# First layer's scan: the output gate of groups 1 to 7 computed as a chain of seven quarter products instead of two full ones

## The reference

```
for l in range(2):                       # 1024 features, 256 + 256 tokens in layer 0
    q, k, v, z, xBC, dt, ga, gs = split(h @ w_in[l])
    x, B, C = silu(dwconv(xBC, conv_w) + conv_b)
    y = ssd_forward(x, dt_f, B, C) + ssd_backward(x, dt_b, B, C) + D * x
    ssd = rmsnorm(y * silu(z), g) @ w_ssd_o        # z: the output gate
```

## Time and profile before

| | |
|---|---|
| median of 3 runs | 2643.51 us (2640.7 to 2645.01) |
| the profiled execution | 2640.4 us, its span 2638.6 us |
| TensorE busy | 98% of the span |
| the first layer's scan | about 446 to 860 us |
| one group of it, where steady | 51.35 us |

### The profile page before, as it was taken

The page is one execution under the profiler, slowest core; times in us unless marked ns, Lnnn a source line. Parts: engine busy times, 40 slices in busy tenths (PEclk is TensorE's granted clock), DMA queues, the critical chain, the costliest instruction groups (busy, mean ns, idle before and its releaser), DMA issues.

```text
span 2638.6 us, 40130 instructions
## 1 busy us (share of the span) xinstructions
PE 2594.3 (98%) x15290; PEld 2042.5 (77%) x15290; DVE 1602.3 (61%) x2659; ACT 788.6 (30%) x1824; POOL 1187.0 (45%) x942
## 2 busy tenths in 40 slices
PE   8999999999999999999999999999999999999998
PEld 7779994555555777888778888876666688899998
DVE  1547835777778577887669660226766744666253
ACT  2430113665656333200021210014555422201210
POOL 4018970333323545457414554401221254586885
PEclk9999999999999999999999999999999999999999
DMA  9347666434341223343455533264443222387654
GB/s 286 97 118 207 183 200 171 112 89 112 105 111 41 57 77 84 95 116 96 110 167 171 157 88 88 88 180 122 108 111 102 65 80 72 88 222 218 169 169 120
DMA packets 519311, 333.12 MB, mean 126 GB/s; under 512 B 15328, under 2 KB 485712, under 8 KB 518864
## 3 DMA queue, kind: packets, MB, share of 16 engines
q1 hardware_dynamic: 507888, 298.19, 40.3%
q0 software_dynamic: 10784, 31.46, 4.8%
q10 hardware_dynamic: 448, 0.89, 0.1%
HBM read 328.11 MB, written 2.38 MB: 125 GB/s over the span
## 4 chain that ended last, share of the span: by engine, by line
PE 92%; DVE 3%; issue 1%; ACT 1%; PEld 1%; DVEq 1%; POOL 0%; PEldq 0%; DMA 0%; ACTq 0%
PE ps L1890 44%; PE ps L1526 24%; PE ps L2263 4%; PE ps L2260 2%; PE ps L2044 2%; PE ps L2021 2%; PE ps L2187 1%; PE ps L2213 1%; PE ps L2081 1%; PE ps L2246 1%; PE ps L2060 1%; PE ps L2069 1%; PE ps L2358 1%; PE ps L1846 1%; PE ps L1552 1%
## 5 line engine op out<-in xcount | busy, mean ns | idle before, releaser
L1526 PE MATMUL ps<-xnT,W 128*128 128x512 f32 (+1 forms) x1760 | 650.6, 525 | 1.8 <-DVE xnT L2516 0.8
L1526 PEld LDWEIGHTS ps<-xnT,W 128*128 128x128 f32 x1760 | 330.0, 190 | 291.1 <-issue 263.7
L929 POOL TENSOR_TENSOR W<-W 128x512 f32<-128x512 f32 x154 | 214.0, 1390 | 612.1 <-DMA W<-in_w_mlp 243.9
L1890 PE MATMUL ps<-TMP,W 128*128 128x128 f32 (+1 forms) x2848 | 482.2, 319 | 1.3 <-DVE TMP L2751 1.2
L1890 PEld LDWEIGHTS ps<-TMP,W 128*128 128x128 f32 x2848 | 422.9, 191 | 32.9 <-DVE TMP L2751 1.3
L1890 PE MATMUL ps<-BIG,W 128*128 128x128 f32 (+1 forms) x2736 | 437.2, 314 | 0.0
L1890 PEld LDWEIGHTS ps<-BIG,W 128*128 128x128 f32 x2736 | 391.4, 191 | 26.7 <-issue 0.7
L1890 PE MATMUL ps<-xnT,W 128*128 128x128 f32 (+1 forms) x2032 | 324.2, 311 | 0.0
L1890 PEld LDWEIGHTS ps<-xnT,W 128*128 128x128 f32 x2032 | 288.7, 191 | 18.9 <-issue 0.8
L1038 ACT ACTIVATE TMP<-ps 128x512 f32<-128x512 f32 (+3 forms) x205 | 91.0, 449 | 569.2 <-PE ps L1890 392.4
L931 POOL TENSOR_TENSOR W<-W 128x512 f32<-128x512 f32 x154 | 219.9, 1428 | 27.4 <-issue 6.0
(11 more groups left out here) (397 smaller groups left out, 3374.5 us busy)
## 6 DMA issues: line engine op xcount, KB each, us to landing
W<-in_w_in SPq DMA_DIRECT2D x188, 512.0 KB, 4.4
W<-in_w_mlp SPq DMA_DIRECT2D x128, 512.0 KB, 4.1
W<-in_ada_w SPq DMA_DIRECT2D x96, 512.0 KB, 4.1
BIG<-cs_rows POOLq DMA_DIRECT2D x96, 256.0 KB, 4.8
W<-in_w_ssd_o SPq DMA_DIRECT2D x32, 512.0 KB, 5.2
W<-in_w_gate SPq DMA_DIRECT2D x22, 512.0 KB, 6.3
W<-in_w_up SPq DMA_DIRECT2D x22, 512.0 KB, 4.5
W<-in_w_down SPq DMA_DIRECT2D x16, 512.0 KB, 3.8
```

Source lines behind the costliest of these rows:

```text
L929: nc.gpsimd.tensor_tensor(w1[:, 0:K, :], wb[:, 0:K, :], wb[:, K:2 * K, :], ALU.add)
L1526: last = mm(dst, w[:, c, 0:m], rhs(k), start=k == 0, stop=k == total - 1)
L1890: done = mm(PS[bank][:, third + half * H:third + half * H + H], w[:, at + c, :], x[:, c, :], start=first and opens and c == 0, stop=last a ...
```

## The change

For layer 0 and groups 1 to 7 the two full products z0 and z1 become seven products of four matmuls each, on token halves and feature halves, 256 columns wide. TensorE runs steps 1 and 2 behind `states(g, 2)`, steps 6, 5 and 7 behind C, and steps 4 and 3 behind `outputs(g, 3)`. B goes where z0 was, and waits for the same convolution. The products use PSUM banks 4 and 5, so the x transposes of the next `turned` wait until these are read. ScalarE copies bank 4 out four times (`gate_copied`) and then takes the silu of both halves in place (`gate_closed`), before `finish(g)`. VectorE adds bank 5 three times (`gate_added`), the last time ahead of the gating of group g's output. GpSimd makes the four weight sums of the next group behind its second DMA of each group (7 times), and once, ahead of the first of them, four sums of token quarters (`gate_tokens`), which are kept where `hT` stands. So the whole of `hT` is written out to DRAM, early in the scan, and its first half is read back too. Each of the seven groups takes two more slots of the ring.

```diff
 def front_order(l, g):
-    return (0, 1, 4, 2, 3, 5) if early_z(l, g) else range(6)
+    return (0, 1, 2, 4, 5, 3) if chained_z(l, g) else range(6)
...
+def gate_keys(g):
+
+    return [("ssd", 0, g, "z0"), ("ssd", 0, g, "z1"), ("zsums", g, 0), ("zsums", g, 1)]
...
-                if key == ("att", 0, 0, "q"):
+                if key == ("ssd", 0, 1, "C"):
                     sp.wait_ge(n_x, scaled_until("down1", KC - 1, 1))
-                    sp.dma_start(h_dram[:, :, :], hT[:, 4:8, :]).then_inc(h_out, 16)
+                    sp.dma_start(h_dram[:, :, :], hT[:, :, :]).then_inc(h_out, 16)
+                if key == quick_keys(MERGE[0] + 6)[0]:
+                    sp.wait_ge(z_ad, gate_adds(NG - 1, 3))
+                    sp.dma_start(hT[:, 0:4, :], h_dram[:, 0:4, :]).then_inc(h_in, 16)
...
+                def gate_tokens():
+
+                    b11, b12, b21, b22 = (xnT[:, 4 * f:4 * f + 4, S * m:S * m + S] for f in range(2) for m in range(2))
+                    t1, t2, t4, t3 = t_gate
+                    pool.wait_ge(n_sh, 8 * NORMS["down1"])
+                    pool.wait_ge(h_out, 16)
+                    nc.gpsimd.tensor_tensor(t1, b12, b11, ALU.subtract).then_inc(z_t, 1)
+                    pool.drain()
+                    nc.gpsimd.tensor_tensor(t2, b22, t1, ALU.subtract).then_inc(z_t, 1)
+                    pool.drain()
+                    nc.gpsimd.tensor_tensor(t4, b21, t2, ALU.subtract).then_inc(z_t, 1)
+                    nc.gpsimd.tensor_tensor(t3, b22, b12, ALU.subtract).then_inc(z_t, 1)
...
+                        if i == 1 and chained_z(l, g + 1) and g < NG - 1:
+                            if g == 0:
+                                gate_tokens()
+                            pool.drain()
+                            sums_of_weights(gate_keys(g + 1), 4, z_ws)
+                            pool.drain()
...
+                def gate_copied(g, step):
+                    gate_done(act, g, step)
+                    if g >= 2 and step == 1:
+                        R("y1", 2 * (g - 2) + 2)
+                    i, m = {1: (0, 0), 6: (0, 1), 7: (1, 1), 4: (1, 0)}[step]
+                    copy(gate_out(g, i, m), PS[4][:, 0:S]).then_inc(z_cp, 1)
+
+                def gate_closed(g):
+                    act.wait_ge(z_cp, gate_copies(g, 4))
+                    act.wait_ge(z_ad, gate_adds(g, 3))
+                    for t in range(2):
+                        z_of = zs[:, g % 2, t, :]
+                        A(z_of, z_of, ACT.Silu).then_inc(ssd["gated"], 1)
...
@@ -1361,28 +1424,39 @@
                     if more:
                         center(g + 1, 0)
                         center(g + 1, 1)
-                        if l == 0:
-                            gated(g + 1, 0)
-                            activated(g + 1, 0)
                     else:
                         R("skip", 2 * NG)
                         keep(0, "q")
                     if l == 0:
                         decays(g, 2)
+                        if more:
+                            center(g + 1, 2)
+                            gate_copied(g + 1, 1)
                         decays(g, 3)
                     if not more:
                         keep(0, "k")
                         keep(0, "v")
-                    if more:
+                    if more and l == 0:
+                        center(g + 1, 3)
+                        gate_copied(g + 1, 6)
+                        activated(g + 1, 0)
+                        activated(g + 1, 1)
+                        gate_copied(g + 1, 7)
+                        activated(g + 1, 2)
+                        gate_copied(g + 1, 4)
+                        activated(g + 1, 3)
+                        if g == NG - 2:
+                            below(NG - 1, 0)
+                        gate_closed(g + 1)
+                    elif more:
                         center(g + 1, 2)
...
+                        for t in range(2):
                             gated(g + 1, t)
...
@@ -1974,19 +2048,54 @@
...
                 def front(g, t, ready=None):
-                    b = 0 if early_z(l, g) and t == 5 else t % 2
-                    if early_z(l, g) and t == 4:
-                        R("conv", 4 * g + 1)
-                    elif early_z(l, g) and t == 5:
-                        R("conv", 4 * g + 3)
-                    elif early_z(l, g) and t == 2:
-                        R("gated", 2 * g + 1)
-                    elif t >= 2:
+                    if t >= 2:
                         R("conv", 4 * g + t - 1)
+                    elif g and chained_z(l, g - 1):
+                        R("conv", 4 * (g - 1) + t + 3)
                     elif g:
-                        R("gated", 2 * (g - 1) + (2 if early_z(l, g - 1) else t + 1))
+                        R("gated", 2 * (g - 1) + t + 1)
                     n = T if t < 3 else nt
-                    product([("ssd", l, g, FRONT[t])], PS[b][:, 0:n], lambda k: xnT[:, k, 0:n], ready=ready)
...
+                    if step == 1:
+                        R("xcd", 3 * g)
+                        R("xc", g)
+                        tile(ka)
+                        times(X, wa[:, 0:4, :], b11, opens=True).then_inc(z_pe, 1)
+                    elif step == 2:
+                        times(Y, wa[:, 4:8, :], b21, opens=True).then_inc(z_pe, 1)
+                    elif step == 6:
+                        pe.wait_ge(z_ws, g)
+                        pe.wait_ge(z_t, 2)
+                        pe.wait_ge(z_cp, gate_copies(g, 1))
+                        give(times(X, w1[:, 4:8, :], t2), ka)
+                    elif step == 5:
+                        pe.wait_ge(z_ad, gate_adds(g, 2))
+                        give(times(Y, w1[:, 0:4, :], t1, opens=True), k1)
+                    elif step == 7:
+                        pe.wait_ge(z_t, 4)
+                        pe.wait_ge(z_cp, gate_copies(g, 6))
+                        times(X, wb[:, 0:4, :], t3).then_inc(z_pe, 1)
+                    elif step == 4:
+                        pe.wait_ge(z_cp, gate_copies(g, 7))
+                        give(times(X, wb[:, 4:8, :], t4), kb)
+                    else:
+                        pe.wait_ge(z_ad, gate_adds(g, 7))
+                        give(times(Y, w2[:, 0:4, :], b22), k2)
...
                 def turned(g):
...
+                    if chained_z(l, g):
+                        pe.wait_ge(z_cp, gate_copies(g, 4))
+                        pe.wait_ge(z_ad, gate_adds(g, 3))
...
@@ -2136,7 +2248,7 @@
                     if more:
                         front(g + 1, 1)
                         if l == 0:
-                            front(g + 1, 4)
+                            front(g + 1, 2)
...
-                    if more:
+                    if more and l == 0:
+                        gate(g + 1, 1)
+                        gate(g + 1, 2)
+                        front(g + 1, 3)
+                        gate(g + 1, 6)
+                        gate(g + 1, 5)
+                        gate(g + 1, 7)
...
                     outputs(g, 1 if l else 3)
-                    if more:
-                        if l:
-                            front(g + 1, 4)
+                    if more and l == 0:
+                        gate(g + 1, 4)
+                        gate(g + 1, 3)
...
+                def gate_added(g, step):
+                    gate_done(dve, g, step)
+                    dve.wait_ge(z_cp, gate_copies(g, {2: 1, 7: 7, 3: 6}[step]))
+                    i, m = {2: (0, 0), 7: (1, 1), 3: (0, 1)}[step]
+                    whole = gate_out(g, i, m)
+                    V.tensor_tensor(whole, PS[5][:, 0:S], whole, ALU.add).then_inc(z_ad, 1)
...
                     if l == 0:
                         masked(g, 2)
+                        if more:
+                            gate_added(g + 1, 2)
                         masked(g, 3)
                     elif not more:
...
                     if more:
                         conv(g + 1, 2)
+                        if l == 0:
+                            gate_added(g + 1, 7)
                         conv(g + 1, 3)
...
                         R("ychunk", n_ch * (g + 1))
                         y = yz[:, 2 * g + t, 0:nt]
                         V.tensor_tensor(y, y, PS[2 + t][:, 0:nt], ALU.add)
+                    if more and l == 0:
+                        gate_added(g + 1, 3)
                     dve.drain()
                     for t in range(2):
                         y = yz[:, 2 * g + t, 0:nt]
```

More of the change, by code:

```diff
@@ L246, with chained_z, gate_copies, gate_adds @@
 FRONT = ("x0", "x1", "B", "C", "z0", "z1")
-def early_z(l, g):
+def chained_z(l, g):
     return l == 0 and g > 0
 def front_order(l, g):
-    return (0, 1, 4, 2, 3, 5) if early_z(l, g) else range(6)
+    return (0, 1, 2, 4, 5, 3) if chained_z(l, g) else range(6)
+def gate_keys(g):
+    return [("ssd", 0, g, "z0"), ("ssd", 0, g, "z1"), ("zsums", g, 0), ("zsums", g, 1)]
+def gate_copies(g, step):
```

(56 more changed lines are left out.)

7 lines of the change are left out of this document (3 added, 4 removed).

## The result

The changed kernel took 2646.07 us (median of 22 runs, 2642.32 to 2648.38) beside 2642.90 us for the kernel before on the same chips: a ratio of 1.0013, interval 1.0007 to 1.0019. So it is slower by 3.2 us, clear of the noise of these runs but less than the 0.2% set above, and 0.8 us above the forecast of 2645.3. The sum came out well; several of its terms did not, and in both directions.

The account below looks back on a forecast made before the run. TensorE, busy throughout a steady group, was taken as the bound, with an equally long chain from the gate's end. Group 0 +4.05, steady groups -3.9, last group +1.6: +1.8 on 2643.5 gives 2645.3 us; 8-in-10 range 2636 to 2652.

Parts of the forecast that it names:

- TensorE's work: Gate product in each of 7 groups: seven narrower products take 12.09 us instead of 13.74, a gain of 1.65 us.
- rival D: Each step of the gate product's chain restarts TensorE, 0.3 us each, seven a group: 14 us more, 2659; chance 0.10.
- The chain at the gate's end: Groups 1 to 6, after the gate's last product: finish and B's wait come 1.0 us later (0.5 to 1.6).
- The weight sums, cover 1.3 us, cost nothing: GpSimd's four sums, groups 1 to 6: mask ready near 634.6, wanted by outputs(g, 1) at 635.9, so no cost.
- rival C: Weight sums hold VectorE in every group, outputs(g, 1) waits 1.8 us six times: in all +12.6 us, 2656; chance 0.12.
- The token sums, +5.7 us in group 0: GpSimd's token and weight sums delay VectorE's masks once, so outputs(0, 1) stalls 5.7 us (0 to 8).
- rival A: GpSimd's sums in group 0 hold VectorE less long, the 5.7 us stall falls away: 2639.6 us; chance 0.15.
- The last group, +1.6 us: Group 7: finish 2.1 us later behind below and two silus, 0.5 us slack, tail 1.6 us later (0.7 to 2.1).

Follow-up runs that it names:

- the spill alone: The kernel before, with only the residual written whole to DRAM and its first half read back six jobs into the merge: 2644.09 us, ratio 0.9999.

## Why the prediction held, and where its terms did not

**TensorE's work** was right. It forecast 1.65 us less in each group; the group without waits lasts 49.46 us, against 51.35 less z0's wait of 0.26 in the kernel before, which is 1.63. No step of the chain restarted TensorE for long (rival D): in the steady groups no wait stands at a line of the gate.

**The chain at the gate's end** was right in size and incomplete in mechanism. I took 1.0 us. B comes 1.25 us late by the trace, where 0.26 + 1.0 was forecast, and its weight load's wait grew by 1.08. By the experiments a group gets 0.33 + 1.00 = 1.33 us back with the whole chain gone, of which 0.26 were there before: 1.07. But I had written that the addition ahead of the multiplications costs nothing more. That holds only while the Silus stand beside it. Alone they were worth 0.33 us, and the addition's place the other 1.00.

**The weight sums, cover 1.3 us, cost nothing** was the step that failed in the steady groups. It rested on sums that begin behind the DMA, 16.6 us into the group (625.8 - 609.25), with 2.3 us of them on VectorE's two-operand operations. The drain kept them until 20.8 us into it (627.79 - 607.02), all four met the masks or the operation behind them and cost 4.0 us, and the cover was overrun: 0.58 us a group, by taking the drain away and by leaving the sums out alike. Over six groups this is 3.5 us that the sum lacked, and why the steady groups gained nothing instead of 3.9 us. The prediction had named a wait at `outputs(g, 1)` as a sign that it is wrong, and that sign came. It is the mechanism of rival C at a third of its size; its length of a sum (2.2 us) was wrong, 1.3 to 1.4 here, and what pushed it over the edge was their place.

**The token sums, +5.7 us in group 0**, failed the other way: no stall, rival A's outcome. But A's reason (VectorE gets several operations in at each drain) held in full at the first drain only. Beside sums with nothing between them VectorE got one operation in for each sum, and mostly two where 0.14 us or more lay between them. Filling that one gap brought a stall of 4.9 us and the group up by 7.2. So the pattern was read nearly rightly and the gap of 2.71 us overlooked, which is as long as ten mask operations. How narrow it was: in the kernel without the second drain the gap was 2.29 us, and a wait of 1.5 came back (group 0 at 51.17). Why the gap differs between kernels (2.26 to 2.71 us) is not shown.

**The last group, +1.6 us**: measured 1.76, made of 0.62 us at the q product, 1.01 and 0.19 at masks, less small change. The forecast had the q product's wait only as its lower bound (0.7) and took 1.6 at the copy that sets the tail; what came on top fell on waits for masks. Its `finish` is 2.6 us behind, as forecast.

**The sum.** Forecast for the scan +1.8 us; measured -1.3 in group 0, nothing in the steady groups, +1.8 in the last: +0.5. Of the two missed terms (5.4 us too dear in group 0, 3.9 too cheap in six groups) most cancels. The kernels' difference is 3.2 us where +1.8 was forecast, and 2.7 of it lie where the forecast had nothing. So the forecast of 2645.3 was near in good part by luck.

**Behind the scan** the forecast had nothing. The second step of attention takes 0.95 us longer in both traces. VectorE there, in the changed kernel:

```profile
854.21 2.16 DVE L3139 TENSOR_TENSOR BIG<-xnT 128x1024 f32<-128x1024 f32 x1
```

GpSimd there, in the changed kernel and then in the kernel before, where the same operation of VectorE started at 854.41 and took 1.22 us:

```profile
852.12 1.75 POOL L960 TENSOR_TENSOR W<-W 128x512 f32<-128x512 f32 x1 [1.00 <-issue]
854.01 1.27 POOL L962 TENSOR_TENSOR W<-W 128x512 f32<-128x512 f32 x1
```

```profile
853.13 1.38 POOL L929 TENSOR_TENSOR W<-W 128x512 f32<-128x512 f32 x1 [1.37 <-issue]
854.65 2.10 POOL L931 TENSOR_TENSOR W<-W 128x512 f32<-128x512 f32 x1
```

GpSimd's next weight sums begin 2.1 us ahead of it now and 1.3 us ahead before, so that VectorE comes second where it came first. Without the drain in the scan the operation takes 1.63 us and the step 8.3 with the same spill, and with the spill alone 1.22 and 7.90, so it is the phase of the two engines and not the traffic. That leaves 3.2 - 0.5 - 0.95 = some 1.7 us of the median's difference, which itself is known to 1.6 us either way. Medians less scan and second step spread over 2.2 us among all kernels here without order. The stretch at half clock in attention could carry it: the two steps that hold it are together 1.9 and 2.0 us longer in the traces of the changed kernel than in the kernel before. But they are 1.6 us longer with the spill alone too, whose median did not move. So this is not shown and stays open.

## What to carry to other kernels

Before a wait is called covered, follow where in time each operation of the other engine will really stand, drains included: a cover of 1.3 us was lost to a start four us later than assumed. When work is taken off a chain, look for the second way of nearly the same length beside it: the close of the gate was worth 0.33 us alone and 1.33 with the addition's place. Here three small edits in three queues (two of them moves, one a drain left out), with the same arithmetic, turned a change that lost 3 us into one that gains 0.33% (2634.55 us beside 2644.01, five runs, ratio 0.9954 to 0.9979).

## What the runs showed of the hardware

A GpSimd drain behind the issue of its own DMA took 4.11 us here (3.01 when one sum of 1.28 us had been put between), though the profile shows no other GpSimd operation in it; without such a DMA ahead it took 0.16 to 0.31. VectorE operations with two SBUF operands beside back-to-back GpSimd operations of 1.3 us lose one us to each of these, and beside five GpSimd operations, two of 2.4 us and three of 1.3, the eight masks took 9.43 us. The Trainium skill (SBUF — State Buffer, "SBUF: two separate sides") has a VectorE operation with two SBUF inputs and a GpSimd operation that reads SBUF exclude each other for the whole of an operation; the 2.42 to 2.44 us that a single mask operation took beside token sums, for 0.35 alone, agree with it. A stall of 4.9 us on TensorE cost 7.2 us in the group: the granted clock fell to the lower of its two levels during the wait, and some 5 us of the work behind it ran there.
